# Hybrid layers: gate products moved among the moba softmax steps, their silu behind them, two output-product units among the last mla steps

## The reference, cut to what matters

```python
h = rms_norm_2(x, norm_g) * (1 + scale) + shift
z = h @ w_in                    # 1024 x 2976
c_q, c_kv, k_rope, g_mla, q_b, k_b, v_b, g_moba = split(z)
o_mla = mla_attention(...)      # 8 heads, q and k of width 96, normalised, rope, causal softmax
o_moba = moba_attention(...)    # 8 heads, width 64, one block of 256 keys, relative bias
y = concatenate([silu(g_mla) * o_mla, silu(g_moba) * o_moba]) @ w_out
return x + gate * y
```

## Time and profile before

| | |
|---|---|
| median of 3 runs | 2108.7 us (2102.17 to 2113.1) |
| the profiled execution, its own time | 2105.32 us |
| its span, first to last instruction | 2103.2 us |
| mean granted TensorE clock | 0.92 |
| PE busy | 1921.8 us, 91% |
| DVE busy | 1583.3 us, 75% |
| ACT busy | 1153.0 us, 55% |

### The profile page before, as it was taken

One profiled execution on the slowest core, in us unless ns is written; L12 is line 12 of the kernel. 1 busy time (PEld: TensorE's weight loads), 2 busy tenths in 40 slices (PEclk: granted clock), 3 DMA queues, 4 the chain that ended last, 5 costly groups with the idle time before them and its releaser, 6 DMA issues.

```text
span 2103.2 us, 25668 instructions
## 1 busy us (share of the span) xinstructions
PE 1921.8 (91%) x9324; PEld 1615.6 (77%) x9324; DVE 1583.3 (75%) x1546; ACT 1153.0 (55%) x1195; POOL 59.8 (3%) x85
## 2 busy tenths in 40 slices
PE   7758979999997799999999999999999998878987
PEld 7648867778785578888888888888888877667766
DVE  6587355788867479988888988888898886656754
ACT  5411214434436466767767776776677665454543
POOL 1000000111010000000000000000000000000000
PEclk9868659999996799999999999999999999969968
DMA  7300004799541379999999999999999973313420
GB/s 254 119 1 1 31 20 160 269 328 328 204 138 43 126 278 379 336 371 348 365 346 360 378 334 372 348 365 345 359 378 336 372 275 109 120 41 114 144 81 20
DMA packets 161947, 489.02 MB, mean 233 GB/s; under 512 B 8178, under 2 KB 13427, under 8 KB 161744
## 3 DMA queue, kind: packets, MB, share of 16 engines
q1 hardware_dynamic: 153536, 458.21, 60.0%
q0 software_dynamic: 8336, 29.81, 4.0%
HBM read 485.36 MB, written 2.62 MB: 232 GB/s over the span
## 4 chain that ended last, share of the span: by engine, by line
PE 70%; DVE 13%; issue 10%; ACT 3%; DMA 3%; POOL 0%; DVEq 0%; ACTq 0%; POOLq 0%
PE bank L1127 19%; PE bank L1129 19%; PE bank L1128 19%; DVE weights_at L1819 2%; PE bank L1305 2%; PE bank L1553 1%; ACT weights_at L2703 1%; PE bank L1618 1%; PE bank L1278 1%; DMA BIG<-in_e_ffn_down 1%; DMA BIG<-in_e_ffn_up 1%; DVE BIG L2120 1%; DMA BIG<-in_e_ffn_gate 1%; PE bank L1293 1%; PE bank L1266 1%
## 5 line engine op out<-in xcount | busy, mean ns | idle before, releaser
L2361 DVE TENSOR_TENSOR expert_weights_low<-BIG,expert_weights_high 128x2048 fp32r<-128x2048 f32 x336 | 750.7, 2287 | 58.5 <-ACT expert_weights_high L2956 58.4
L2956 ACT ACTIVATE expert_weights_high<-BIG 128x2048 fp32r<-128x2048 f32 x336 | 626.2, 1922 | 72.6 <-DMA BIG<-in_o_moe_up 38.5
L1127 PE MATMUL bank<-expert_weights_high,expert_x_high 128*128 128x512 f32 x896 | 351.5, 392 | 3.0 <-DVE expert_x_low L2426 2.9
L1129 PE MATMUL bank<-expert_weights_low,expert_x_high 128*128 128x512 f32 x896 | 349.0, 389 | 0.0
L1128 PE MATMUL bank<-expert_weights_high,expert_x_low 128*128 128x512 f32 x896 | 348.8, 389 | 0.0
L1819 DVE TENSOR_TENSOR weights_at<-BIG,weights_at 128x2048 fp32r<-128x2048 f32 (+2 forms) x100 | 219.1, 2191 | 96.2 <-ACT weights_at L2703 94.4
L2703 ACT ACTIVATE weights_at<-BIG 128x2048 fp32r<-128x2048 f32 (+2 forms) x100 | 183.6, 1836 | 177.9 <-DMA BIG<-in_e_ffn_gate 35.7
L1127 PE MATMUL bank<-weights_at,x_high 128*128 128x512 f32 (+2 forms) x608 | 246.5, 405 | 25.1 <-DVE weights_at L1819 12.5
L1128 PE MATMUL bank<-weights_at,x_low 128*128 128x512 f32 (+2 forms) x608 | 240.9, 396 | 0.0
L1129 PE MATMUL bank<-weights_at,x_high 128*128 128x512 f32 (+2 forms) x608 | 240.3, 395 | 0.0
L1127 PEld LDWEIGHTS bank<-expert_weights_high,expert_x_high 128*128 128x128 f32 x896 | 168.3, 188 | 37.3 <-DVE expert_x_low L2426 3.0
(11 more groups left out here) (398 smaller groups left out, 2425.5 us busy)
## 6 DMA issues: line engine op xcount, KB each, us to landing
BIG<-in_o_moe_gate SPq DMA_DIRECT2D x112, 1024.0 KB, 5.2
BIG<-in_o_moe_up SPq DMA_DIRECT2D x112, 1024.0 KB, 5.6
BIG<-in_o_moe_down SPq DMA_DIRECT2D x112, 1024.0 KB, 5.3
BIG<-in_w_ada POOLq DMA_DIRECT2D x48, 512.0 KB, 5.0
BIG<-in_w_in SPq DMA_DIRECT2D x20, 1024.0 KB, 5.0
BIG<-in_o_w_qkv SPq DMA_DIRECT2D x12, 1024.0 KB, 5.0
BIG<-in_e_w_in SPq DMA_DIRECT2D x10, 1024.0 KB, 5.6
BIG<-in_e_ffn_gate SPq DMA_DIRECT2D x10, 1024.0 KB, 5.2
```

The costliest lines, as they stand in the source:

```text
L1127: mm(b, high_l, high_r, start=start, stop=False, skip_group_check=not check)
L1129: last = mm(b, high_l, low_r, start=False, stop=stop, skip_group_check=not check)
L2361: tt_(E_WL[q % E_SLOTS], half(q % E_SLOTS), E_WH[q % E_SLOTS].bitcast(F32), SUB).then_inc(w_low, 1)
L2956: f(E_WH[q % E_SLOTS], half(q % E_SLOTS), ACT.Copy).then_inc(w_high, 1)
```

## The change

1. The four units of chunk 1 and the four of chunk 5 (`GATE_UNITS`) leave their places ahead of the steps. Units 0 and 1 stand behind `mobaT`; units 2 to 7 stand in turns 0 to 5, between scores(i + 2) and weights_transposed(i). All go to banks 5 (tile 0) and 7 (tile 1).
2. ScalarE reads these banks with Copy as they are filled (turns 0, 1, 4, 5), and makes the Silu of both gates from SBUF in turn 8, two instructions, ahead of weights_out(8).
3. The mla transposes move from between the halves of chunk 5 to the head of TensorE's turn 6, through banks 5 and 7 alone. Both readers take them in turn 6: ScalarE behind exponentials(7), VectorE behind masked(7) and sums_inverted(6).
4. VectorE's turning and scaling of mla queries and keys goes from ahead of the steps into turns 0, 2 and 3. Its scratch buffer moves.
5. Splits of weight halves move: `low` from turns 4, 5 to 1, 5, 7, `high` from turns 2, 3 to 0, 4, 5, one of each remaining ahead of the steps. The ring of buffers leaves out one pair from the fifth pair of halves on.
6. weights_transposed uses bank 4 alone and values bank 6 alone, where each had two.
7. The moba outputs are gated in turn 9 instead of 8, and transposed in turn 11 instead of 10.
8. Of w_out, the two units (0, 1) stand in turns 14 and 15, the product (1, 1) behind the steps, and the transposes of the mla outputs behind that product instead of ahead of it.

```diff
+GATE_UNITS = [(c, j, m) for c in (1, 5) for j in range(2) for m in range(2)]
 # the plan of the banks
-        z_chunk(1)
         for u in range(4):
             add(("mobaT", l, u), "av"[u % 2], 4 + u)
-        for u in range(8):
-            add(("mlaT", l, u), "av"[u % 2], 4 + u % 4)
-        z_chunk(5)
...
         for i in range(17):
+            if i == 6:
+                for u in range(8):
+                    add(("mlaT", l, u), "av"[u % 2], 5 + 2 * (u % 2))
...
+            if i < 6 and GATE_UNITS[i + 2][1]:
+                add(("z", l, GATE_UNITS[i + 2][0], GATE_UNITS[i + 2][2]), "a", 5 + 2 * GATE_UNITS[i + 2][2])
             if i < 16:
-                add(("pair", l, "weightsT", i), "a", 4 + i % 2)
+                add(("pair", l, "weightsT", i), "a", 4)
             if i:
-                add(("pair", l, "values", i - 1), "v", 6 + (i - 1) % 2)
+                add(("pair", l, "values", i - 1), "v", 6)
...
-        halves.place(Z_PAIRS + BASE_PAIRS)
+        halves.place((Z_PAIRS + BASE_PAIRS) * 2 + [Z_PAIRS[0]] + BASE_PAIRS + [Z_PAIRS[0]])
-        ROT2 = R(19264, 1024).rearrange("p (i m g w) -> p i m g w", i=4, m=TT, w=16)
+        ROT2 = R(21312, 1024).rearrange("p (i m g w) -> p i m g w", i=4, m=TT, w=16)
 # TensorE
                 z_chunk(4)
-                z_chunk(1)
                 pe.wait_ge(qk_ready, 2 * l + 2)
                 to_channels(("mobaT", l), 4, ...)
-                z_chunk(5, mla_heads)
+                gate_unit(0)
+                gate_unit(1)
                 wait_taken(pe, ("mobaT", l, 2))
                 wait_taken(pe, ("mobaT", l, 3))
                 scores(0)
                 scores(1)
                 for i in range(17):
                     if i == 6:
+                        mla_heads()
                         wait_taken(pe, ("mlaT", l, 6))
                         wait_taken(pe, ("mlaT", l, 7))
                     if i < 14:
                         scores(i + 2)
-                    if i == 10:
+                    if i < 6:
+                        gate_unit(i + 2)
+                    elif i == 11:
                         gated_to_channels((2, 3))
+                    elif i in (14, 15):
+                        if i == 14:
+                            wait_taken(pe, ("yT", l, 3))
+                        out_product(0, 1, (i - 14,))
                     if i < 16:
                         weights_transposed(i)
                     if i:
                         values(i - 1)
-                wait_taken(pe, ("yT", l, 3))
-                out_product(0, 1)
+                out_product(1, 1)
                 gated_to_channels((0, 1))
-                out_product(1, 1)
                 wait_taken(pe, ("yT", l, 1))
                 out_product(0, 0)
                 out_product(1, 0)
 # VectorE
                 z_out(4)
-                mla_scaled()
-                low(2)
+                mla_sums()
                 for u in (1, 3):
                     ... # reads mobaT
-                for u in range(1, 8, 2):
-                    ... # reads mlaT
+                low()
                 masked(0)
                 for i in range(16):
                     if i < 15:
                         masked(i + 1)
                     sums_inverted(i)
+                    if i == 6:
+                        for u in range(1, 8, 2):
+                            ... # reads mlaT
+                    elif i == 11:
+                        x_out(("yT", l), units=(2, 3))
                     if i:
                         values_out(i - 1)
-                    if i in (4, 5):
+                    if i == 0:
+                        mla_turned(0)
+                    elif i == 2:
+                        mla_scaled()
+                    elif i == 3:
+                        mla_turned(1)
+                    elif i in (1, 5, 7):
                         low()
-                    elif i == 8:
-                        heads_gated(512, ZGB, 5)
-                    elif i == 11:
-                        x_out(("yT", l), units=(2, 3))
+                    elif i == 9:
+                        heads_gated(1, 512, ZGB)
 # ScalarE
+                def gates_out():
+
+                    for g0 in (ZGB, ZG):
+                        A(f(ZB[:, :, g0:g0 + 512], ZB[:, :, g0:g0 + 512], ACT.Silu), gate_silu)
...
                 root(3 * l + 3, qk_sums, qk_roots, s_qk[:, 0:32])
-                high(2)
-                z_out(1)
                 for u in (0, 2):
                     ... # reads mobaT
-                for u in range(0, 8, 2):
-                    ... # reads mlaT
-                z_out(5)
+                high()
                 exponentials(0)
                 for i in range(16):
                     if i < 15:
                         exponentials(i + 1)
+                    if i < 6:
+                        gate_out(i)
+                    elif i == 6:
+                        for u in range(0, 8, 2):
+                            ... # reads mlaT
+                    elif i == 8:
+                        gates_out()
+                    elif i == 11:
+                        x_out(("yT", l), units=(2, 3))
                     weights_out(i)
-                    if i in (2, 3):
+                    if i in (0, 4, 5):
                         high()
-                    elif i == 10:
-                        x_out(("yT", l), units=(2, 3))
                 x_out(("yT", l), units=(0, 1))
                 high(4)
```

More of the change, by code:

```diff
@@ L299, in z_chunk @@
             for m in range(TT):
-                add(("z", l, c, m), "a" if c in (1, 5) else "av"[m], 2 * (Z_ORDER.index(c) % 2) + m)
+                add(("z", l, c, m), "av"[m], 2 * (Z_ORDER.index(c) % 2) + m)
         def pair_scores(i):
@@ L624, in build @@
         o_ready = sem("o_ready")
+        gate_silu = sem("output_gates_ready")
         moe_in = sem("moe_input_ready")
@@ L1662, in z_chunk, with gate_unit, mla_heads @@
                     by_token(("z", l, c), ("z", l, c), HEAD0 if c == 0 else BANK, ready)
-                def mla_heads(j):
-                    if j == 0:
-                        return
+                def gate_unit(n):
+                    c, j, m = GATE_UNITS[n]
+                    unit(("z", l, c), j, m)
+                def mla_heads():
                     pe.wait_ge(mla_ready, l + 1)
@@ L1724, in _, with out_product @@
                 out_banks = {}
-                def out_product(c, j):
+                def out_product(c, j, tiles=range(TT)):
                     high, low = split_half(pe, ("wo2", l, c, j))
-                    for m in range(TT):
+                    for m in tiles:
                         if j:
@@ L2574, in mla_scaled @@
                     V(tt_(keys, keys, bc(roots[:, :, 8:16], 3, [P, TT, 8, 96]), MUL))
-                    mla_turned(1)
                 def masked(i):
@@ L3055, in z_out, with gate_out @@
                     c0, n = (0, HEAD0) if c == 0 else (HEAD0 + (c - 1) * BANK, BANK)
-                    for m in range(TT if c in (1, 5) else 1):
-                        A(f(ZB[:, m, c0:c0 + n], take(act, ("z", l, c, m))[:, 0:n],
-                            ACT.Silu if c in (1, 5) else ACT.Copy), ea)
+                    A(f(ZB[:, 0, c0:c0 + n], take(act, ("z", l, c, 0))[:, 0:n], ACT.Copy), ea)
+                def gate_out(i):
+                    c, j, m = GATE_UNITS[i + 2]
+                    if j:
+                        c0 = HEAD0 + (c - 1) * BANK
+                        A(f(ZB[:, m, c0:c0 + BANK], take(act, ("z", l, c, m)), ACT.Copy), ea)
+                def gates_out():
+                    for g0 in (ZGB, ZG):
+                        A(f(ZB[:, :, g0:g0 + 512], ZB[:, :, g0:g0 + 512], ACT.Silu), gate_silu)
                 def moba_squares(q):
@@ L3123, in _ @@
                     A(f(QKTB[:, 2 * u:2 * u + 2, :], b, ACT.Copy, scale=prm("moba_columns", 2 * l + u // 2)), ea)
-                for u in range(0, 8, 2):
-                    b = take(act, ("mlaT", l, u)).rearrange("p (g t) -> p g t", g=2)
-                    A(f(QKT2[0:96, 2 * u:2 * u + 2, :], b[0:96], ACT.Copy, scale=prm("mla_columns", 2 * l + u // 4)[0:96]), ea)
-                z_out(5)
+                high()
                 exponentials(0)
@@ L3131, in _ @@
                         exponentials(i + 1)
+                    if i < 6:
+                        gate_out(i)
+                    elif i == 6:
+                        for u in range(0, 8, 2):
+                            b = take(act, ("mlaT", l, u)).rearrange("p (g t) -> p g t", g=2)
+                            A(f(QKT2[0:96, 2 * u:2 * u + 2, :], b[0:96], ACT.Copy,
+                                scale=prm("mla_columns", 2 * l + u // 4)[0:96]), ea)
+                    elif i == 8:
+                        gates_out()
+                    elif i == 11:
+                        x_out(("yT", l), units=(2, 3))
                     weights_out(i)
-                    if i in (2, 3):
+                    if i in (0, 4, 5):
```

(2 more changed lines are left out.)

25 lines of the change are left out of this document (13 added, 12 removed).

## The result

| | before | after |
|---|---|---|
| median of the timed runs | 2105.43 us, 4 runs | 2131.66 us, 4 runs (2128.88 to 2132.28) |
| profiled execution, its own time | 2105.32 | 2128.88 |
| its span | 2103.2 | 2126.7 |

The ratio is 1.0116, with a 95% interval of 1.0092 to 1.0140: slower by 1.2%, some 24 us. The forecast was 2126, slower, in a range of 2100 to 2143.

What follows compares the result with a forecast made beforehand. TensorE was taken as the bound over most of the program, hand-overs as the bound of the steps. Layer 0 +10.6 and layer 1 +8.5, together +19 on 2105.3, gave 2124.4, by the median 2127.8; taken 2126, range 2100 to 2143.

Steps and rivals of the forecast that it cites:

- The start of the steps: Behind mobaT: TensorE idles 5.0 us for VectorE's late read, yet scores(2) leads its old place by 18.9 us.
- Steps 0 to 5: Turns with gate units: 4.2 us of TensorE each, waits of 1.3 ahead of scores(5) and 1.8 ahead of scores(7).
- Six turns: Steps 0 to 5: six turns and two waits, 1817.6 + 24.8 + 3.1 = 1845.5 for the end of values(4).
- Turn 6: Mla transposes: first read of bank 5 5.6 us behind values(4), four rounds 5.6 us, scores(8) at 1856.7; lead gone.
- Turns 8 and 9: ScalarE between exponentials(9) and (10): Silu with two table loads 4.7 us, 3.0 of it new on the path.
- The end: Steps' end and w_out: TensorE waits 5.5 us ahead of product (0, 0) for VectorE's half; 2.4 us half clock.
- Layer 1: Second hybrid layer: 116.2 us against 114.1 in layer 0, half of that the gap that goes; +8.5 us.
- the span ahead of 1801: Sign: the prediction is wrong if the span before 1801 changes.
- Cold moba steps: Rival, moba steps: half clock stays, units cost 5.2 instead of 2.8 us, three per layer; 2140 us; chance 0.16.
- The clock stays up throughout: Rival: full clock everywhere, mla steps too; +2.9 in layer 0, +0.8 in layer 1; 2109 us; chance 0.18.
- TensorE becomes the bound: Rival, moba steps: waits of 1.3, 1.8 and 5.6 us go, clock stays up; 2092 us; chance 0.14.
- Dearer switches: Rival, ScalarE: table loads in running work cost twice their row; four new ones add 5.1 us; 2131; chance 0.07.

Runs made afterwards that it cites:

- The front experiment: Changed kernel with VectorE reading mobaT ahead of the sum of squares and ScalarE ahead of the roots; 2117.24 us, ratio 1.0058.
- the run with Exp's table early: Changed kernel with the three reorderings (tail, turn 6, front), Silu at the end of turn 7, and a 128x1 Exp ahead of exponentials(0); 2101.03 us, ratio 0.9988.
- The run without it: Changed kernel with both Silu instructions replaced by Copy, so that both table loads are gone; 2134.21 us, ratio 1.0143.
- the w_out part alone: Kernel before, with only w_out units (0, 1) in turns 14 and 15 and product (1, 1) ahead of the mla output transposes; 2105.41 us, one run.
- The tail experiment: Changed kernel with the transposes of the mla outputs put back ahead of product (1, 1); 2121.94 us, ratio 1.0091.
- front and turn 6: Edits to the changed kernel: mobaT read ahead of sums and roots (alone 2117.24 us); mlaT read ahead of masked(7) and exponentials(7) (alone 2127.03 us).
- the last run: The run with Exp's table early, plus gate unit 2 ahead of the turns, later units one turn earlier, ScalarE's reads in the plan's order; 2101.71 us, ratio 0.9989.
- the run with the Silu in turn 7 and the reorderings: Changed kernel with the three reorderings (tail, turn 6, front) and the Silu at the end of ScalarE's turn 7; 2109.44 us, ratio 1.0030.

## Why the prediction was right, point by point

The waits were right and the speed between them was too good; that the total came close is in part luck, as told below the points. Layer 0, from the start of mobaT, forecast (its half clock of 2.4 us put where it fell) and measured:

| | forecast | measured |
|---|---|---|
| scores(2) | 18.5 | 18.4 |
| end of values(4) | 46.4 | 50.0 |
| scores(8) | 57.6 | 63.4 |
| end of the steps | 98.9 | 103.9 |
| product (0, 0) starts | 110.9 | 115.9 |
| w_out ends | 124.5 | 129.4 |

1. *The start of the steps*: forecast 5.0 us of idle time and a lead of 18.9; 4.58, and a lead of 16.4 with the half clock in it. The front experiment takes this wait away, and 7.1 / 6.3 us go.
2. *Steps 0 to 5*: the waits of 1.3 and 1.8 are 1.14 and 1.60. This is where the forecast failed in size: 27.9 us for this stretch, measured 31.6. The step was "Six turns" of 4.2 us with half clock on one product alone (its four terms add up to 4.3). The idle 3.11 us ahead of scores(2), which the forecast had in its marks (1814.9 to 1817.6) and not in its clock, came with the clock down a second time: the unit behind it took 5.3 us for 2.8, and the first turn 6.5 for 3.6, +2.9. The other five, at full clock, took 22.4 us for 21.2, about 4.5 each (scores 0.63 for 0.45, transposes 0.44 for 0.35), +1.2; the shorter waits give 0.4 back.
3. *Turn 6*: the first read of bank 5 came 5.7 us behind values(4), forecast 5.6, and TensorE waited 5.41. The four rounds took 7.6, forecast 5.6: a fill costs about 1.0 us there, not 0.46, with the clock at 0.50. In the run with Exp's table early, layer 0, where these transposes ran at full clock, the same four rounds took 5.9. This is the second term of that kind, +2.0.
4. *Turns 8 and 9*: the forecast had 3.0 us for the Silu. The run without it gained nothing, and 1.3 us at the spot. The stretch still came out as forecast (40.4 against 41.3), so something else is in it: the w_out part alone makes this stretch 37.6 in the kernel before, and leaves 2.8. It stands ahead of scores(15), where the w_out part changes nothing: from scores(8) to scores(11) it is 9.1 us for 11.6 before, from there to scores(13) 10.4 for 6.4 (9.1 without the Silu's loads), and to scores(15) 8.4 for 6.7. VectorE's `low` of 2.29 us, new in turn 7 ahead of masked(9), and the single banks are candidates; neither was tried alone, and this stays open.
5. *The end*: 5.5 forecast, 5.40 measured, and 2.1 of half clock behind it, forecast 2.4. The tail experiment took 4.3 / 4.7 off the tail, and the w_out part alone shows the wait in the old kernel.
6. *Layer 1*: +8.5 forecast, +12.2 measured, with the same waits and the same slow unit behind scores(2). The forecast took off the whole 2.1 us by which layer 1 had been longer, while its sentence speaks of half of that.

The two layers together are +27.9 where the forecast had +19. The device's time shows +24, since what lies ahead of the layers was 4.3 us shorter in the profiled execution after. That is the luck in the number: the layers grew by 8.9 us more than forecast, and half of this was hidden by a stretch that the change doesn't touch. From kernel to kernel the first product of layer 0 stands anywhere from 1738.1 (the tail) to 1753.7 (the front), with the same program ahead of it.

Of the signs, the idle times, the table loads and the early scores(2) (16.4 and 18.3 us) came as told, with 5.3 us between exponentials(9) and (10) instead of 6. Two did not. scores(8) was to stand within 3 us of its old place and stood 10.0 and 7.6 behind it: the terms of points 1 to 3. And the span ahead of 1801 was not to change; it moves by more than 4.3 us by itself, so that this sign could not tell anything.

The rivals. *Cold moba steps* (2140) fell as told: not three units more at half clock but one; its kind of loss, though, is 4.5 of the 4.9 us that were missing in layer 0. *The clock stays up throughout* fell: 0.86, 0.79 and 0.87. *TensorE becomes the bound* fell with the waits in the trace: the program order that it had against it held. With that order changed (front and turn 6) scores(8) comes 10.3 / 10.1 us earlier, at 107.6 / 105.5 against 107.9 / 108.0 before: even then the six units gain 0.3 / 2.5 us of the 16.8 that they take (2.8 / 4.9 in the last run). *Dearer switches* fell: the two loads in turn 8 take 1.28 us each, and nearly nothing stands beside them.

```profile
1869.96 1.28 ACT L3089 ACT_TABLE_LOAD   x1
1871.26 2.14 ACT L3089 ACTIVATE BIG<-BIG 128x1024 f32<-128x1024 f32 x2
1873.43 0.38 ACT L3118 ACTIVATE BIG<-bank 128x256 f32<-128x256 f32 x1
1873.84 1.28 ACT L3107 ACT_TABLE_LOAD   x1
1875.13 0.46 ACT L3107 ACTIVATE BIG<-bank,SM 128x128 f32<-128x128 f32 x1
```

The Trainium skill ("ScalarE: Activation LUTs", What ACT_TABLE_LOAD costs) gives 1.38 us of drain with each switch; here the Silu starts 1.30 us behind the start of its load and the Exp 1.29 behind the start of its own, and the measurement decides.

## What to carry to other kernels

Work moved into a stalled stretch pays only if its operands, its banks and its readers are free there: follow each added unit to who must empty the bank first, and where that reader stands in its own program order. Price a wait ahead of dense products with the slow matmuls that can follow it, in the kernel after 1.6 to 2.6 us each time, behind waits of 3.1 to 5.4 us, and read idle time for a piece to be moved in the very kernel that it is moved in.

## What the runs showed of the hardware that was not expected

An ACT_TABLE_LOAD started only once the wait of the activation that needed it was over: at 1862.06 behind 0.84 us of idle time in the run with the Silu in turn 7 and the reorderings, ahead of exponentials(0) behind 3.00 us in the same run, and behind 6.65 in the kernel after (1813.42). None of these loads was hidden by the wait ahead of it; an Exp of 128x1 ahead of it costs 0.20 us and hides the whole 1.28. And matmuls whose output nobody uses made the kernel 5.6 / 2.7 us a layer faster than waiting did.

The length of one wait doesn't tell whether the clock falls. In the run with Exp's table early, the gate unit of turn 5 stands behind the same idle time of 1.58 us in both layers, and takes 4.5 us in layer 0 and 2.9 in layer 1; what differs between them is open.
